# A trunk kernel's mixer begins with the attention values by token tile, half of it inside the normalisation

## The reference, cut to what matters

```python
for l in range(DEPTH):                                   # DEPTH = 2
    m = token_mixer(x, w_in[l], ...)
    x = layer_norm(ALPHA * x + m, ln1_g[l], ln1_b[l])
    f = swiglu(...) if l % 2 == 0 else moe_swiglu(...)   # dense, then 8 experts with 2 chosen
    x = layer_norm(ALPHA * x + f, ln2_g[l], ln2_b[l])
# token_mixer: hcat = x @ w_in; its columns are q (512), kv (768: k and v, each for the
# compressed, the selected and the window branch), attention gates (24), three conv inputs,
# four retention inputs and the merge gates.
# nsa_compress: gelu(blocks of 32 tokens @ cmp_w1 + b1) @ cmp_w2 + b2, for k and for v
```

## The kernel before

| s | before | after |
|---|---|---|
| 0 | k and v for compression | attention values V |
| 1 | q, first half | k and v for compression |
| 2 | compression 0 | q, first half |
| 3 | q, second half | compression 0 |
| 4 | compression 1 | q, second half |
| 5 | attention keys k | compression 1 |
| 6 | compression 2 | attention keys k |
| 7 | V | compression 2 |
| 8 | compression 3 | compression 3 |
| 9 | attention gates (half a tile's work) | attention gates |

## Time and profile before

### The profile page before, as it was taken

The page is one execution under the profiler, slowest core; times in us unless marked ns, Lnnn a source line. Parts: engine busy times, 40 slices in busy tenths (PEclk is TensorE's granted clock), DMA queues, the critical chain, the costliest instruction groups (busy, mean ns, idle before and its releaser), DMA issues.

```text
span 1836.8 us, 29509 instructions
## 1 busy us (share of the span) xinstructions
PE 1814.7 (99%) x10873; PEld 1588.5 (86%) x10877; DVE 1457.4 (79%) x1675; ACT 1177.8 (64%) x1441; POOL 56.2 (3%) x37
## 2 busy tenths in 40 slices
PE   9999999999999999999999999999999999999996
PEld 8999998999989999997888888888888888888885
DVE  6675677545576766768999999999998998999998
ACT  6544444444447444446778787787787877877875
POOL 0000000000000000002001001010010010100100
PEclk9999999999999999999999999999999999999998
DMA  9544454555536343455999999999999999999994
GB/s 387 194 167 149 161 184 184 184 183 183 185 138 273 138 161 138 170 189 204 386 375 356 378 358 371 373 342 393 365 358 379 356 376 374 339 389 368 361 376 176
DMA packets 72222, 510.67 MB, mean 278 GB/s; under 512 B 8144, under 2 KB 8528, under 8 KB 11360
## 3 DMA queue, kind: packets, MB, share of 16 engines
q1 hardware_dynamic: 69264, 498.15, 71.5%
q10 hardware_dynamic: 1424, 6.32, 0.9%
q0 software_dynamic: 1472, 5.31, 0.9%
HBM read 507.65 MB, written 2.10 MB: 278 GB/s over the span
## 4 chain that ended last, share of the span: by engine, by line
PE 96%; DMA 2%; DVE 1%; SPq 0%; issue 0%; ACT 0%; POOL 0%; POOLq 0%; DVEq 0%
PE PS L411 19%; PE PS L413 19%; PE PS L412 19%; PE PS L384 10%; PE PS L385 10%; PE PS L386 10%; PE PS L842 1%; DMA raw<-wstream 1%; PE PS L573 1%; PE PS L605 1%; PE PS L397 1%; PE PS L398 1%; PE PS L399 1%; PE PS L588 1%; DMA G<-x_rows,rows 0%; PE PS L886 0%
## 5 line engine op out<-in xcount | busy, mean ns | idle before, releaser
L1298 DVE TENSOR_TENSOR w_lo<-raw,w_hi 128x1024 fp32r<-128x1024 f32 x471 | 576.1, 1223 | 221.9 <-ACT w_hi L930 220.5
L930 ACT ACTIVATE w_hi<-raw 128x1024 fp32r<-128x1024 f32 x471 | 498.8, 1059 | 275.3 <-PE PS L413 204.4
L1301 DVE TENSOR_TENSOR w_lo<-raw,w_hi 128x1024 fp32r<-128x1024 f32 x471 | 574.4, 1220 | 0.0
L931 ACT ACTIVATE w_hi<-raw 128x1024 fp32r<-128x1024 f32 x471 | 492.9, 1046 | 0.0
L411 PE MATMUL PS<-w_hi,xT_hi 128*128 128x512 f32 x960 | 381.6, 398 | 0.0
L384 PE MATMUL PS<-xT_hi,w_hi 128*128 128x256 f32 x1312 | 376.5, 287 | 0.3 <-DVE w_lo L1301 0.3
L412 PE MATMUL PS<-w_lo,xT_hi 128*128 128x512 f32 x960 | 374.7, 390 | 0.0
L413 PE MATMUL PS<-w_hi,xT_lo 128*128 128x512 f32 x960 | 374.5, 390 | 0.0
L385 PE MATMUL PS<-xT_lo,w_hi 128*128 128x256 f32 x1312 | 371.5, 283 | 0.0
L386 PE MATMUL PS<-xT_hi,w_lo 128*128 128x256 f32 x1312 | 371.3, 283 | 0.0
L384 PEld LDWEIGHTS PS<-xT_hi,w_hi 128*128 128x128 f32 x1312 | 251.5, 192 | 7.1 <-issue 5.1
(11 more groups left out here) (265 smaller groups left out, 1565.2 us busy)
## 6 DMA issues: line engine op xcount, KB each, us to landing
raw<-wstream SPq DMA_DIRECT2D x471, 1024.0 KB, 6.7
soft<-ln ACTq DMA_DIRECT2D x4, 1024.0 KB, 6.1
X<-x SPq DMA_DIRECT2D x2, 512.0 KB, 4.1
raw<-wstream SPq DMA_DIRECT2D x2, 512.0 KB, 6.7
x_rows<-X ACTq DMA_DIRECT2D x1, 1024.0 KB, 5.0
cst<-consts SPq DMA_DIRECT2D x1, 962.5 KB, 15.0
out<-X ACTq DMA_DIRECT2D x1, 512.0 KB, 3.2
out<-X ACTq DMA_DIRECT2D x2, 256.0 KB, 2.0
```

The source lines that it names most:

```text
L930: activate(w_hi[:, at % RING, 0:SUB // 2], src[:, 0:SUB // 2], ACT.Copy).then_inc(half_done, 1)
L931: activate(w_hi[:, at % RING, SUB // 2:SUB], src[:, SUB // 2:SUB], ACT.Copy).then_inc(hi_done, 1)
L1298: v.tensor_tensor(w_lo[:, at % RING, 0:SUB // 2], src[:, 0:SUB // 2], w_hi[:, at % RING, 0:SUB // 2], ALU.subtract)
L1301: v.tensor_tensor(w_lo[:, at % RING, SUB // 2:SUB], src[:, SUB // 2:SUB], w_hi[:, at % RING, SUB // 2:SUB], ALU.subtract).then_inc(lo_done, 1)
```

## The change

The values' weights become tile 0, and the order of the head is as in the table's last column. V is computed with tokens as rows, so its first token tile needs only the first token tile of `xT`: `first_tokens(n, slot, 0)` issues its 16 high-side matmuls (`xT_hi` by `w_hi`, `xT_hi` by `w_lo`) ahead of the second token tile's transposes, at n = 0 and at n = 2. The 16 matmuls of the second token tile and the 16 of `xT_lo` follow after them (`first_tokens_low`). Fillers: at n = 0, six in place of two; at n = 2, five and four around the 16 matmuls in place of sixteen. The fillers and `NORM_BANKS` use other banks, so that bank 0 is free for the tile. SP loads x's second half behind the two halves of tile 0. ACT drains the first token tile at once (n = 0 and 2); at n = 0 it splits tile 0 ahead of the second token tile's drains, and DVE's four parts move ahead of its third `xT_lo`.

```diff
-NORM_BANKS = (0, 1, 6, 7)
+NORM_BANKS = [(2, 3, 6, 7)] * 3 + [(0, 1, 6, 7)]
-TOKEN_UNITS = (4, 16, 17)
+TOKEN_UNITS = (0, 16, 17)
-HEAD = {0: 0, 1: 1, 3: 2, 5: 3, 7: 4, 9: 5}
-COMPRESS = (2, 4, 6, 8)
+HEAD = {0: 0, 1: 1, 2: 2, 4: 3, 6: 4, 9: 5}
+COMPRESS = (3, 5, 7, 8)
@@ SP
-            for t in range(TT):
-                sp.dma_start(X[:, t, :], x[t * P:(t + 1) * P, :]).then_inc(x_in[t], 16)
+            sp.dma_start(X[:, 0, :], x[0:P, :]).then_inc(x_in[0], 16)
             for c in range(2):
                 at = slice(c * SUB // 2, (c + 1) * SUB // 2)
                 sp.dma_start(raw[:, 0, at], wstream[0][:, at]).then_inc(landed[0] if c else part_in, 16)
+            sp.dma_start(X[:, 1, :], x[P:T, :]).then_inc(x_in[1], 16)
@@ PE
+            def first_tokens(n, slot, t, ready=None):
+                pe.wait_ge(xT_hi_rdy, 2 * TT * n + 2 * t + 2)
+                o, tok = PS[:, PA[0], t * T:(t + 1) * T], slice(t * P, (t + 1) * P)
+                for k in range(DK):
+                    if ready:
+                        ready(k)
+                    at = slice(k * 2 * P, (k + 1) * 2 * P)
+                    mm(o, xT_hi[:, k, tok], w_hi[:, slot, at], start=(t == 0 and k == 0), stop=False,
+                       skip_group_check=True)
+                    mm(o, xT_hi[:, k, tok], w_lo[:, slot, at], start=False, stop=False, skip_group_check=True)
...
+            def first_tokens_low(n, slot):
+                for t in range(TT):
...
+                        last = mm(o, xT_lo[:, k, tok], w_hi[:, slot, k * 2 * P:(k + 1) * 2 * P], start=False,
+                                  stop=(t == TT - 1 and k == DK - 1), skip_group_check=True)
+                return last
@@ PE, to_features
-                            stay_busy(2)
+                            stay_busy(6, PA[1])
+                            first_tokens(0, 0, 0, first_part)
                         pe.wait_ge(x_in[t], 16)
...
-                        stay_busy(9 if n == 3 else 16)
+                            stay_busy(9)
+                        elif n == 2:
+                            stay_busy(5, PA[1])
+                            sub_ready(LAYER)
+                            first_tokens(2, LAYER % RING, 0)
+                            stay_busy(4, PA[1])
+                        else:
+                            stay_busy(16, PA[1])
...
-                stay_busy(3 if n else 8)
+                stay_busy(3 if n else 8, SB if n == 3 else PA[1])
@@ PE, tile 0 of a mixer
-                        if l:
-                            sub_ready(base)
-                        first_unit(2 * l, PA[0], base % RING, None if l else first_part).then_inc(sub_used, 1)
+                        first_tokens(2 * l, base % RING, 1)
+                        first_tokens_low(2 * l, base % RING).then_inc(sub_used, 1)
@@ ACT, norm
-                for b in range(4 if n < 3 else 0):
+                    if n == 2 and t == 0:
+                        high(n, 0)
+                        high(n, 1)
+                if n == 0:
+                    high(n, 0)
+                    high(n, 1)
+                    split_first()
+                for b in range(0 if n == 1 else 2, 4 if n < 3 else 0):
                     high(n, b)
@@ ACT, after(s)
-                    if s in (1, 3):
+                    if s in (2, 4):
-                    elif s == 0:
+                    elif s == 1:
...
-                    elif s == 5:
+                    elif s == 6:
@@ DVE, norm
-                        if n == 0 and b == 2:
+                        if n == 0 and b == 1:
                             for c in range(4):
                                 first_part(c)
@@ host
-        subs += [first[2], first[0], compress[0], first[1], compress[1], first[3], compress[2], first[4], compress[3],
+        subs += [first[4], first[2], first[0], compress[0], first[1], compress[1], first[3], compress[2], compress[3],
                  first[5]]
```

More of the change, by code:

```diff
@@ L441, in last_pair, with first_part, stay_busy @@
                         last.then_inc(tok_ps, 1)
-            def stay_busy(n):
+            def first_part(k):
+                if k % 2 == 0:
+                    pe.wait_ge(part_rdy, k // 2 + 1)
+            def first_tokens(n, slot, t, ready=None):
[10 more added lines that the diff above has]
+                for t in range(TT):
+                    o, tok = PS[:, PA[0], t * T:(t + 1) * T], slice(t * P, (t + 1) * P)
+                    for k in range(DK):
+                        if k % 4 == 0:
+                            pe.wait_ge(xT_rdy, 2 * TT * n + 2 * t + k // 4 + 1)
+                        last = mm(o, xT_lo[:, k, tok], w_hi[:, slot, k * 2 * P:(k + 1) * 2 * P], start=False,
+                                  stop=(t == TT - 1 and k == DK - 1), skip_group_check=True)
+                return last
+            def stay_busy(n, bank=SB):
                 for _ in range(n):
-                    mm(PS[:, SB, :], identb, cb[:, 0:512], start=True, stop=True)
+                    mm(PS[:, bank, :], identb, cb[:, 0:512], start=True, stop=True)
             def to_features(n):
@@ L463, in to_features @@
                             pe.wait_ge(norm_rdy, 2 * TT * (n - 1) + 2 * t + k // 4 + 1)
-                        last = nc.tensor.transpose(PS[:, NORM_BANKS[2 * t + k // 4], (k % 4) * P:(k % 4 + 1) * P],
+                        last = nc.tensor.transpose(PS[:, NORM_BANKS[n][2 * t + k // 4], (k % 4) * P:(k % 4 + 1) * P],
                                                    X[:, t, k * P:(k + 1) * P], ident)
@@ L502, in compress @@
                     if s == COMPRESS[0]:
-                        pe.wait_ge(dve_free, unit_count(NU - 1, "dve") * l + 1)
+                        pe.wait_ge(dve_free, unit_count(NU - 1, "dve") * l + unit_count(1, "dve"))
                     slot = (base + s) % RING
@@ L960, in high @@
                 activate(xT_hi[:, 4 * c:4 * c + 4, t * P:(t + 1) * P],
-                         PS[:, NORM_BANKS[b], :].rearrange("p (k t) -> p k t", k=4), ACT.Copy).then_inc(xT_hi_rdy, 1)
+                         PS[:, NORM_BANKS[n][b], :].rearrange("p (k t) -> p k t", k=4), ACT.Copy).then_inc(xT_hi_rdy, 1)
             def load_norm(n):
@@ L974, in after @@
                     sub = OUT0 > s >= BRANCH0
-                    if not (s in (0, 1, 3, 5, 8, 9, 10, 11, 15, 20, 21, 22, 23) or sub):
+                    if not (s in (1, 2, 4, 6, 8, 9, 10, 11, 15, 20, 21, 22, 23) or sub):
                         return
                     act.wait_ge(hi_done, base + s + RING)
-                    if s == 0:
+                    if s == 1:
                         if l == 0:
@@ L988, in after @@
                     act.wait_ge(sub_used, base + s + 1)
[L989 to L990 removed]
+                    if s in (2, 4):
+                        c = s - 2
                         activate(qT[:, c:c + 2], pa(HEAD[s]), ACT.Copy).then_inc(act_free, 1)
[L992 removed]
+                    elif s == 1:
                         for g in range(NG):
@@ L995, in after @@
                                 activate(z[par * DH:(par + 1) * DH, 0, :, g].rearrange("p v r q -> p v q r"),
-                                         pa(0)[g * DH:(g + 1) * DH, :, par::2].rearrange("p v (q r) -> p v q r", r=8),
+                                         pa(1)[g * DH:(g + 1) * DH, :, par::2].rearrange("p v (q r) -> p v q r", r=8),
                                          ACT.Copy).then_inc(z_hi_rdy, 1)
-                    elif s == 5:
+                    elif s == 6:
                         for g in range(NG):
                             for half in range(2):
-                                last = activate(kT[half * DH:(half + 1) * DH, :, g, :], pa(3)[g * DH:(g + 1) * DH],
+                                last = activate(kT[half * DH:(half + 1) * DH, :, g, :], pa(4)[g * DH:(g + 1) * DH],
                                                 ACT.Copy)
@@ L1374, in norm @@
                         at = (slice(None), slice(4 * c, 4 * c + 4), slice(t * P, (t + 1) * P))
-                        v.tensor_tensor(xT_lo[at], PS[:, NORM_BANKS[b], :].rearrange("p (k t) -> p k t", k=4),
+                        v.tensor_tensor(xT_lo[at], PS[:, NORM_BANKS[n][b], :].rearrange("p (k t) -> p k t", k=4),
                                         xT_hi[at], ALU.subtract).then_inc(xT_rdy, 1)
-                        if n == 0 and b == 2:
+                        if n == 0 and b == 1:
                             for c in range(4):
@@ L1445, in after @@
                                 "p (q r) -> p q r", r=8), hi, ALU.subtract)
-                    if s in (0, 7, 12, 13, 14, 15, 16, 17, 18, 19):
+                    if s in (0, 1, 12, 13, 14, 15, 16, 17, 18, 19):
                         dve.wait_ge(sub_used, base + s + 1)
-                    if s == 0:
+                    if s == 1:
                         for g in range(NG):
@@ L1453, in after @@
                                 dve.wait_ge(z_hi_rdy, 5 * l + 2 * g + 3)
```

(6 more changed lines are left out.)

6 lines of the change are left out of this document (1 added, 5 removed).

## The result

The changed kernel takes 1843.26 us, median of 6 runs (1842.21 to 1844.04), against 1837.13 us before (6 runs, 1835.89 to 1837.65): a ratio of 1.0035, 95% interval 1.0025 to 1.0044. It is slower by 6.1 us, 0.35%. The profiled execution took 1843.95 us with a span of 1842.1.

What follows compares the result with a forecast made beforehand. PE's queue was taken to bound the kernel (busy 99% of the span). Terms 1.4 - 0.5 + 5.2 - 1.7 = +4.4 us on the median of 1837.3 gave 1841.7, range 1839.2 to 1844.4; slower at 0.66.

Steps and rivals of the forecast that it cites:

- start, second tile: Start of the first mixer: transposes and fillers now queue behind half a tile, second tile at 17.8 for 16.40, +1.4 us.
- gap ahead of the keys at 32: First mixer, PE's wait ahead of the keys for a tile late by DMA: goes in the new order, -0.5 us.
- wait ahead of the gates' tile, first mixer: PE runs out 3.75 us behind the keys; tile 9, rounded behind the kT copies, starts 6.26 behind: +2.6 us.
- the same, second mixer: Second mixer, the same PE wait for the gates' tile behind the keys and two compression tiles: +2.6 us.
- clock behind the waits: Behind the gates' tile waits: nothing in the sum; rival (8%) that the clock falls, 3.4 us each, 1845.1 or 1848.5.
- n = 2: At n = 2, 16 matmuls and fillers go into PE's wait for DVE's X, tile 0 ends earlier: -1.7 us.
- ahead of the router: Sum of the start, gap, two waits and n = 2 terms: +4.4 us.
- a dearer start: Rival (12%) at the start: tile 0's first half lands at 8.4 as before, +2.3 in place of +1.4, 1842.6 us.

Runs made afterwards that it cites:

- the first experiment: The changed kernel with ACT rounding tile 9 (the gates' weights) ahead of the copies of the keys to kT in both mixers: 1838.36 us, ratio to before 1.0006.

## Why the prediction was right, and where it was off

It said 1841.7 in a range of 1839.2 to 1844.4, slower; 1843.26 lies inside. The moved median is 6.1 against 4.4 forecast. By its own steps, from the profiles:

| term | forecast | measured |
|---|---|---|
| start, second tile | +1.4 | +1.7 (18.14 - 16.40) |
| gap ahead of the keys at 32 | -0.5 | -0.6, no wait there |
| wait ahead of the gates' tile, first mixer | +2.6 | +2.7 |
| the same, second mixer | +2.6 | +2.9 |
| clock behind the waits | 0 | +1.5 (4.47 - 2.97), first mixer |
| n = 2 | -1.7 | -1.6 (5.94 - 7.56) |
| ahead of the router | +4.4 | +6.6 |

The column's sum is the shift of PE's work ahead of the router, where the first transpose starts at 835.65 and not 829.05. The shorter stretch at the lower level there gave the profiled execution some 1.4 back, hence 5.3 between the two spans. That stretch is not a matter of the change alone (3.4 or 6.8 us, as told above), and the medians, at 6.1, are the better measure.

That the number lies inside the range is in part luck. The range was to leave out nearly all of the clock's fall, and the room that took it was meant for a dearer start.

**Start.** Mechanism right: with transposes and fillers behind half a tile, what had been under the wait for weights was in the queue. The term was 0.3 short in this execution. x's first half landed 0.2 later, so the first transposes began at 5.18 and not 4.99. ACT's parts began at 7.79, right behind its drain, and then at 9.11 with a wait for the load, where I had 7.5 and 8.55; DVE's began at 8.45, where I had 8.20. This execution is the latest of the six profiles with this start: in the five others the second tile begins at 17.61 to 17.89, around the 17.8 forecast. Putting the start back moved the second tile by 1.6, and loading x first cost 0.84 in the trace, so SP's new order is right by itself and the order on PE is what costs.

**The waits.** The largest term, read off rows of before in which nobody waited, came out as forecast in the first mixer, 51.18 - 44.92 = 6.26 us behind the keys. In the second it was 6.55, since ACT's copies began 0.54 behind the first compression matmul and not 0.26, in both profiles of the changed kernel; why is open. Two experiments, one of ACT's order and one of the tiles', show the cause and exclude that the tiles' shortness alone makes the waits.

**The clock.** This is the step that failed. I held it as a rival at 8%, with 3.4 us a fall. I put it into the sum at nothing. It fell behind the first wait in both profiles of the changed kernel, for 3.4 us at the lower level, which costs 1.5; my price came from the router's 6.8 us. My argument against was the 1.51 us wait at 544 that left the clock alone; the new wait is over 1 us longer, and that row could not bear the conclusion. The rule of the Trainium skill that I set beside it ("TensorE: Matmul & The Clock Gate", HAM oscillation: waits between bursts make PE start cold again) pointed the right way; here the trace agrees with it in the first mixer and not in the second. That section of the Trainium skill tells it of DMA waits of some 3 to 5 us, longer than both waits here. Nor did the router bear it out as I wrote: in the first experiment's profile the clock fell there too, at 839.5, while PE went through 16 matmuls of 16 columns (838.09 to 840.38) and the 0.85 us wait behind them did not occur. What makes the clock fall in the first mixer and not in the second stays open. With fillers in the waits the median came out at 4.0 above before; the table's other terms give 5.1, and 4.6 with that profile's earlier start, which is where its work stands ahead of the router (833.60 against 829.05).

**n = 2.** As forecast in size and place; ACT's square root was not delayed, and the undone change took the 1.6 back.

## What to carry to other kernels

When tiles are reordered, take for each tile the time from the end of the last one that holds its buffer to its own readiness, with the drains that stand ahead of it in the queue. Hold it against the work that now lies between. A chain that no one waits for before is the first to look at. A drain that is wanted late should stand behind the rounding that is wanted soon. Where the change opens a new idle stretch on PE, give the clock's fall a price and a real chance. To start work early pays only where what it pushes back was not hidden.

## What the runs showed of the hardware

PE idle for 2.6 us in the first mixer was followed by 3.4 us at 0.53 to 0.55 of the clock in both profiles of the changed kernel; 2.9 us of idle in the second mixer, by none. Ten fillers of 2.33 us in the same place kept 1.00. So the length of the idle time alone does not decide it, and the same wait can cost 2.7 or 4.2 us.

At the router the fall was 3.4 or 6.8 us long, in no profile anything between, and in the first experiment it came among small matmuls with no wait of PE next to it. Two kernels that differ at the start alone can show either length: 3.4 with x loaded first, 6.8 with six fillers more.

A load that takes the place of another does not take its landing time. Tile 0's first half, moved one place up, needed 6.2 us to land in the first profile and 5.4 to 5.9 in the six others with this order, where x's second half of the same size had needed 4.5 from that place. It landed between 7.0 and 7.8 us, and I had taken 6.1 to 7.1.
